# Several waits of TensorE re-arranged at once in a hybrid attention and PEER layer: unrolled head loop, early merge, low halves in quarters, turned choices and h2, the turn of stages 2 and 3

## The reference, cut to what matters

```python
h = rms_norm(x);  z = h @ w_in                    # 2048 -> 9216: GLU a, b, q, k, v, two gates
conv = swish(layer_norm(depthwise_conv31(a * sigmoid(b)))) @ w_conv_out
attn = rms_norm((softmax(q1 k1) - lam * softmax(q2 k2)) @ v) @ w_attn_out     # 8 heads
x = x + (sigmoid(gate_c) * conv + sigmoid(gate_a) * attn) @ w_out
h2 = rms_norm(x)                                  # PEER: 16384 experts of one neuron
idx, sc = top16(top16(q1 . k1) + top16(q2 . k2))  # 8 retrieval heads, 128 x 128 keys
a = einsum("td,thkd->thk", h2, u_tab[idx]);  w = softmax(sc) * gelu(a)
x = x + einsum("thk,thkd->td", w, v_tab[idx])
```

## Time and profile before

| | before |
|---|---|
| three runs, us | 4312.8, 4311.2, 4311.3 (median 4311.3) |
| profiled execution, us | 4312.25 |
| its span, us | 4310.4 |
| mean granted clock of TensorE | 0.972 |
| busy: PE | 4110.0 us, 95% |
| busy: VectorE, GpSimd, ScalarE | 3034.5 (70%), 1442.5 (33%), 1060.9 (25%) |
| DMA | 1225.88 MB, mean 284 GB/s |

### The profile page before, as it was taken

The page is one execution under the profiler, slowest core; times in us unless marked ns, Lnnn a source line. Parts: engine busy times, 40 slices in busy tenths (PEclk is TensorE's granted clock), DMA queues, the critical chain, the costliest instruction groups (busy, mean ns, idle before and its releaser), DMA issues.

```text
span 4310.4 us, 69663 instructions
## 1 busy us (share of the span) xinstructions
PE 4110.0 (95%) x25286; PEld 4014.7 (93%) x25286; DVE 3034.5 (70%) x4447; ACT 1060.9 (25%) x1090; POOL 1442.5 (33%) x682
## 2 busy tenths in 40 slices
PE   8999999999989998999999999999889999999999
PEld 7888888898889998999999999999889999999999
DVE  6876777778756423677637877877468878787874
ACT  3222222222212112222213223232212222222221
POOL 3333232332323332444423333333523323332310
PEclk9999999999999999999979999999999999999999
DMA  7988979979968986866637787778687877777763
GB/s 287 319 310 321 331 273 337 342 261 320 347 223 268 344 309 219 305 224 235 208 137 303 309 317 305 301 309 319 263 315 280 305 287 296 289 294 289 294 255 128
DMA packets 444255, 1225.88 MB, mean 284 GB/s; under 512 B 32800, under 2 KB 256800, under 8 KB 343968
## 3 DMA queue, kind: packets, MB, share of 16 engines
q1 hardware_dynamic: 374224, 881.46, 58.0%
q0 software_dynamic: 36864, 268.45, 15.1%
q10 hardware_dynamic: 32976, 73.47, 4.4%
HBM read 1007.54 MB, written 349.95 MB: 315 GB/s over the span
## 4 chain that ended last, share of the span: by engine, by line
PE 53%; issue 29%; POOL 9%; DVE 6%; DMA 1%; ACT 0%; SPq 0%; POOLq 0%; DVEq 0%; ACTq 0%
PE ST L1710 27%; PE ST L1626 18%; POOL w_lo L551 7%; PE PA L1626 3%; POOL w_lo L543 2%; PE ST L1685 2%; PE PA L1404 2%; PE PA L1636 1%; DVE wk L1234 1%; DMA w_raw<-w_all 1%; DVE cand L1204 1%; DVE wk L1238 0%; DVE isel L1242 0%; DVE ti L1200 0%; DVE wk L1196 0%
## 5 line engine op out<-in xcount | busy, mean ns | idle before, releaser
L624 ACT ACTIVATE w_hi<-w_raw 128x2048 fp32r<-128x2048 f32 x368 | 703.5, 1912 | 1458.5 <-PE ST L1710 786.7
L543 POOL TENSOR_TENSOR w_lo<-w_raw,w_hi 128x2048 fp32r<-128x2048 f32 x133 | 623.8, 4690 | 1154.8 <-ACT w_hi L624 1154.8
L1710 PE MATMUL ST<-wt_hi,w_hi 128*128 128x416 f32 x2048 | 719.4, 351 | 23.3 <-DVE wt_lo L1319 12.7
L1710 PE MATMUL ST<-wt_hi,w_lo 128*128 128x416 f32 x2048 | 724.4, 354 | 0.0
L1710 PE MATMUL ST<-wt_lo,w_hi 128*128 128x416 f32 x2048 | 716.4, 350 | 0.0
L551 POOL TENSOR_TENSOR w_lo<-w_raw,w_hi 128x512 fp32r<-128x512 f32 x280 | 371.4, 1357 | 774.3 <-ACT w_hi L624 774.3
L1404 PE MATMUL PA<-h_hi,w_hi 128*128 128x272 f32 x2496 | 549.4, 302 | 17.8 <-issue 11.8
L581 POOL DMA_INDIRECT rows<-v_rows,v_idx x128 | 312.7, 2443 | 729.5 <-DVE PA L1330 720.8
L1626 PE MATMUL ST<-h_hi,w_hi 128*128 128x416 f32 x1408 | 532.9, 379 | 11.8 <-POOL w_lo L543 11.8
L1404 PE MATMUL PA<-h_hi,w_lo 128*128 128x272 f32 x2496 | 530.0, 295 | 0.0
L1404 PE MATMUL PA<-h_lo,w_hi 128*128 128x272 f32 x2496 | 528.8, 294 | 0.0
(11 more groups left out here) (242 smaller groups left out, 6731.9 us busy)
## 6 DMA issues: line engine op xcount, KB each, us to landing
w_raw<-w_all SPq DMA_DIRECT2D x368, 1024.0 KB
u_in<-w_all SPq DMA_DIRECT2D x128, 1024.0 KB, 8.5
u_rows<-u_out SPq DMA_DIRECT2D x512, 256.0 KB, 7.4
v_rows<-w_all SPq DMA_DIRECT2D x128, 1024.0 KB, 9.1
a_scr<-gb ACTq DMA_DIRECT2D x128, 208.0 KB
g_scr<-g_st ACTq DMA_DIRECT2D x26, 1024.0 KB, 4.4
a_st<-a_scr SPq DMA_DIRECT2D x16, 1664.0 KB
gl_st<-g_scr SPq DMA_DIRECT2D x16, 1664.0 KB, 16.0
```

The source lines that it names most:

```text
L543: pool.tensor_tensor(w_lo[:, slot, :], raw[:, slot, :], w_hi[:, slot, :].bitcast(F32), ALU.subtract)\
L624: act.activation(w_hi[:, slot, :], raw[:, slot, :], ACT.Copy).then_inc(hi_ready, 1)
L1710: last = mm(PD[k], a, r_[b][:, c, :], start=(c == 0 and y == 0), stop=(c == GRP - 1 and y == 2))
```

## The change

1. **Head loop.** TensorE's loop over head pairs and its loops of the merge are written out; its program grows from 5264 rows to 7945. On VectorE a head's last eviction (`evac(hp, r, 8)`) goes ahead of its `o_norm`.
2. **Merge.** The first merge unit does both its tiles for heads 0 to 6, then both for head 7. The first part waits for the eviction of the last `z` unit and the norms of seven heads, the second for the last norm. Head 7's low half is read from `o_lo_st` in place, so one load is gone; the mean stands behind the unit.
3. **Low halves.** All low halves of GpSimd but the first two are made in quarters.
4. **Choices.** `choices_t` stands behind k = 10, `gate_sums` behind k = 3.
5. **Turn of h2.** 64 passes of 128 columns in place of 256 of 32, in two halves, behind unit 40 and in unit 41, into ST. ScalarE copies each half into PA in four operations, for which TensorE waits before the second half and before the rounds.
6. **Turn of stages 2 and 3.** `load_ag(0)` is cut in four parts that stand between the weight loads. Of the last low halves VectorE makes the odd ones and GpSimd the even ones, with 3, 4 and 4 fetches ahead; the `prep` stand between. x2 is no longer loaded ahead of stage 3: group 0 copies its results, x2 is added in group 14 through `gb` (16 loads, `residual`), and in the gather columns at the end (`xg_res`). The row additions of `v` move by three slots.

The diff, cut to its core:

```diff
@@ sync: end of the head loop, end of stage 2, stage 3
-            sp.dma_start(o_lo[:, NH - 1, :].bitcast(F32), o_scr[NH - 1]).then_inc(o_loaded[1], 16)
...
-            load_ag(0)
-            pq_pu_loads(g_end, (NQ + NU) // 2)
+            def load_ag_part(n):
+
+                c, b = slice(2 * n, 2 * n + 2), slice(n * NGB // 4, (n + 1) * NGB // 4)
+                sp.dma_start(a_st[:, c, :], a_scr[c, :, 0:NT].rearrange("c p n -> p c n")).then_inc(ag0_loaded, 16)
+                sp.dma_start(gl_st[:, b, :, :].rearrange("p b c n -> p b (c n)"),
+                             g_scr[b, :, 0:GRP, :].rearrange("b p c n -> p b (c n)")).then_inc(ag0_loaded, 16)
+
+            assert g_end + 3 == (NQ + NU) // 2
+            for v in range(g_end, g_end + 3):
+                for n in range(2):
+                    if 2 * (v - g_end) + n < 4:
+                        load_ag_part(2 * (v - g_end) + n)
+                    sp.wait_ge(lo_ready, v * 2 + (n + 1 + U_PQ))
+                    load_w(v + (U_PQ // 2 + 1), n)
...
-                if n == 0:
-                    sp.wait_ge(unit_done, NZ + NO + NQ + NU)
-                if n < 2:
-                    for i in (2 * n, 2 * n + 1):
-                        sp.dma_start(acc[:, 4 * i:4 * i + 4, :], x2_scr[4 * i:4 * i + 4].rearrange("c p n -> p c n"))\
-                            .then_inc(acc_loaded[i], 16)
+            sp.wait_ge(unit_done, NZ + NO + NQ + NU)
+            sp.dma_start(xg_res[:, :, :], x2_scr[:, :, NT:T].rearrange("c p n -> p c n")).then_inc(xg_loaded, 16)
@@ gpsimd
-            with pool.Fori(1, NZ // 2) as v:
-                for n in range(2):
-                    lo4(v * 2 + n, n)
-            with pool.Fori(NZ // 2, U_PU // 2 + 1) as v:
-                for n in range(2):
-                    lo(v * 2 + n, n)
+            with pool.Fori(1, U_PU // 2 + 1) as v:
+                for n in range(2):
+                    lo(v * 2 + n, n, v * 6 + (3 * n - 3))
...
-            w = U_PU + U_G0 + BU * NGB + 1
-            while w < U_PV + 2:
+            for w, n in ((U_PV - 6, 3), (U_PV - 4, 4), (U_PV - 2, 4), (U_PV, 0)):
+                for i in range(n):
+                    fetch(j)
+                    j += 1
                 pool.wait_ge(lo_ready, w)
-                lo(w, w % 2)
-                w += 1
-                for i in range(2):
-                    if j < SLOTS:
-                        fetch(j)
-                        j += 1
+                nth += 3
+                lo(w, w % 2, nth)
@@ scalar: after the eviction of units 40 and 41
+                act.wait_ge(h2t_ready, n + 1)
+                for q in range(4):
+                    act.activation(PA[:, q, n * 256:n * 256 + 256].rearrange("p (k j) -> p k j", j=32),
+                                   ST[:, 2:4, :].rearrange("p a (k j) -> p (a k) j", j=P)[:, :, 32 * q:32 * q + 32], ACT.Copy)\
+                        .then_inc(h2t_taken, 1)
@@ vector: head loop, rounds, end of stage 2, stage 3
+                    evac(hp, r, 8)
                     o_norm(h)
                     if r == 0:
                         turn(hp, next(turns))
-                    evac(hp, r, 8)
...
-            dve.wait_ge(h2g_ready, 1)
+            dve.wait_ge(h2t_taken, 8)
...
-            for i in range(SLOTS - NGB // 2 * DOTS):
-                dot(NGB // 2, i)
+            for w, dots, preps in ((U_PV - 7, range(0, 3), ()), (U_PV - 5, range(3, 7), ()), (U_PV - 3, range(7, tail), range(0, 3)),
+                                   (U_PV - 1, (), range(3, 8))):
+                split(w, w % 2)
+                if preps and preps[0] == 0:
+                    dve.wait_ge(ag0_loaded, 128)
+                for c in preps:
+                    prep(0, c)
+                for i in dots:
+                    dot(NGB // 2, i)
+            split(U_PV + 1, 1)
@@ tensor: head loop, merge, turn of h2, choices
-            with pe.Fori(0, NH // 2) as hp:
+            for hp in range(NH // 2):
...
+            for ks in (range(KC - 1), range(KC - 1, KC)):
+                for t in range(2):
+                    if ks[0] == 0 and t == 1:
+                        pe.wait_ge(zb_full, NZ + 2)
+                    elif ks[0] > 0 and t == 0:
+                        pe.wait_ge(norm_done, 3 * NH + 1)
+                    for k in ks:
+                        for a, b, f, y in last_head(k):
+                            last = mm(PV[t][:, f, :], a[:, 0, (KC * t + k) * P:(KC * t + k + 1) * P], b,
+                                      start=(k == 0 and y == 0), stop=(k == KC - 1 and y == 2))
+            mean()
+            merge_unit(0, 1, 0, o_hi, o_lows)
...
-                for k in range(KD):
-                    for q in range(4):
-                        for y, src in enumerate((h2_hi, h2_lo)):
-                            last = mm(PA[:, q, 32 * k:32 * k + 32], src[:, k, NT:T].bitcast(F32), ident[:, 32 * q:32 * q + 32],
-                                      start=(y == 0), stop=(y == 1))
-                last.then_inc(h2g_ready, 1)
+                if half == 0:
+                    pe.wait_ge(oh_ready, 1)
+                else:
+                    pe.wait_ge(h2t_taken, 4)
+                for k in range(KD // 2):
+                    for y, src in enumerate((h2_hi, h2_lo)):
+                        last = mm(ST[:, 2 + k // 4, k % 4 * P:(k % 4 + 1) * P], src[:, half * (KD // 2) + k, NT:T].bitcast(F32), ident,
+                                  start=(y == 0), stop=(y == 1))
...
-                u_unit(v_end, 0, UA, {3: choices_t} if tt else None)
-                u_unit(v_end, 1, UA, {1: gate_sums} if tt == TT - 1 else None)
+                u_unit(v_end, 0, UA, {10: choices_t} if tt else None)
+                u_unit(v_end, 1, UA, {3: gate_sums} if tt == TT - 1 else None)
...
-            u_unit(TT * TOPK_UNITS // 2, 1, PD, {KD - 1: h2_turned})
+            u_unit(TT * TOPK_UNITS // 2, 1, PD, {KD - 3: lambda: h2_turned(1)})
+            pe.wait_ge(h2t_taken, 8)
```

More of the change, by code:

```diff
@@ L1334, in _ @@
             own.by(V.memset(acc_g, 0.0))
-            dve.wait_ge(al_loaded, 16)
-            dve.wait_ge(gl_loaded, 16)
-            for c in range(GRP):
-                prep(0, c)
             dve.wait_ge(a_g_ready, 1)
@@ L1343, in _, with group @@
             dve.wait_ge(lo_ready, U_PV + 2)
-            def group(g, parity, more, slots, splits, pre=None):
+            def group(g, parity, more, slots, splits, pre=None, first=False, last=False):
                 s0, rounds, n_slots = slots
@@ L1366, in group @@
                         split(g * GRP + (n + U_PV + 2), n % 2)
-                    if n == GRP - 1 and n_slots > GRP:
+                    if last:
+                        residual(2 * n)
+                        residual(2 * n + 1)
+                    if n == GRP - 1 and n_slots > GRP and not first:
                         gather_add(s0, parity * PER_GRP + GRP, rounds)
             rounds_per = 2 * PER_GRP // NG
-            with dve.Fori(0, NGRP // 2 - 1) as v:
+            group(0, 0, True, (0, 0, PER_GRP - NG), GRP, first=True)
+            group(1, 1, True, (-NG, -1, PER_GRP), GRP)
+            with dve.Fori(0, NGRP // 2 - 2) as v:
                 own.loop(v, 4 * GRP)
                 for b in range(2):
-                    group(v * 2 + b, b, True, (v * (2 * PER_GRP), v * rounds_per, PER_GRP), GRP)
-            own.endloop(NGRP // 2 - 1)
-            done = (NGRP // 2 - 1) * 2 * PER_GRP
+                    group(v * 2 + (b + 2), b, True, (v * (2 * PER_GRP) + (2 * PER_GRP - NG), v * rounds_per + (rounds_per - 1), PER_GRP), GRP)
+            own.endloop(NGRP // 2 - 2)
+            done = (NGRP // 2 - 1) * 2 * PER_GRP - NG
             def hand_over():
```

103 lines of the change are left out of this document (66 added, 37 removed).

## The result

| | before | after |
|---|---|---|
| runs, us | 4312.8, 4311.2, 4311.3, 4317.85 | 4209.0, 4223.6, 4219.7, 4201.8 |
| median, us | 4312.05 | 4214.35 |
| profiled execution, us | 4312.25 | 4208.99 |
| span, us; mean granted clock | 4310.4; 0.972 | 4206.9; 0.984 |

The ratio is 0.9761 with an interval of 0.9744 to 0.9777. Forecast were 4214 us, and 4180 to 4248. The total is right; the parts show that this is partly luck, as misses of either sign cancel. The runs of the changed kernel lie 22 us apart, those of before 7: one more thing to explain.

The account below looks back on a forecast made before the run. TensorE was taken to bound the kernel, busy 4110.0 of 4310.4 us, so the sum is one of stalls plus the turn of h2: -16 - 14 + 20 - 20 - 36 - 31 = -97, from 4311.3 to 4214 us, range 4180 to 4248.

Parts of the forecast that it names:

- Point 1: Head loop: writing it out removes three waits for instructions and their slow clock; late `o_norm` gives back 2 us; minus 16.
- Point 2: Merge: begun with seven heads, 84 of 96 matmuls stand ahead of what needs the last head; minus 14 us.
- I charge 3 us: Start of the merge: TensorE wants the first gated tile at about 1222.5 and gets it at about 1225.
- Point 3: Low halves in quarters: GpSimd and VectorE take turns, so low halves come late in the top-k stage; plus 20 us.
- Point 4: Top-k stage: choices at k = 10, seven steps later, remove four waits for `isel` and their slow clock; minus 20 us.
- Point 5: Turn of h2: 64 passes of 128 columns replace 256 of 32, with a 4 us wait for ScalarE; minus 36 us.
- rival (c): Turn of h2 stays at half clock by the skill's transpose rule: 6.7 us more and some, 4222 us; chance 0.05.
- Point 6: Turn of stages 2 and 3: loads in parts, `prep` between dots, recover most of 41 us lost; minus 31 us.
- Rival (b): End of stage 2 stays bound by DMA: 15 to 20 us more, 4232 us; chance 0.14.
- (a): Top-k stage: low halves in quarters keep up, so their cost is 0; time 4194 us; chance 0.22.
- (d): Head loop: written out, instruction fetching still waits at each head pair; time 4230 us; chance 0.05.
- (e): Rounds of stage 2: quartered low halves come late, making the kernel slower, 4339 us at 11 us each; chance 0.03.

Follow-up runs that it names:

- the last kernel: Changed kernel with low halves whole from the first w_out unit on, last dots ahead of the prep, and load_ag(1) in four parts: median 4192.4 us, ratio 0.97.

## Why the prediction was right, point by point

| point | forecast, us | first profile | mean of profiles |
|---|---|---|---|
| 1 head loop | -16 (10 to 18) | -15.9 | -16.2 (of two before) |
| 2 merge, seven heads | -14 (9 to 18) | | -9.6 (one pair) |
| 3 quarters, top-k | +20 (0 or 20) | +14.2 | +19.9 |
| 3 quarters, merge | none | | -11.0 (one pair) |
| 4 choices | -20 (16 to 20) | | -21.3 (one pair) |
| 5 turn of h2 | -36 (32 to 42) | -38.5 | -38 |
| 6 turn of stages (236 to 248) | -31 (16 to 35) | -24.1 | -22.6 |
| 6 stage 3 proper (from 248) | none | +2.1 | +6.1 |

The last column adds up to -92.7, with +1 for the rest, where the ratios say -103 and -95.

**Point 1** held in its mechanism and size. The written-out code is fetched without a wait. That the eviction ahead costs the heads 2 us can't be seen: 1125.1 us with it behind is inside the range with it ahead. The two profiles with the loop as before (1134.2, 1140.3) lie 6 us apart, so the size is known to a few us only.

**Point 2** was right about the place: the stretch shrank by 15.4 us, 1.4 more than forecast, and the last norm's end was covered. But the step "I charge 3 us" for the gates took the stretch for the stage. VectorE's work is a chain of its own here, and TensorE caught up with it: without quarters 9.6 us are left of it at the end of the merge. With quarters in place its parts came to 4.8 us for the seven heads and 3.9 for the eviction, by one profile each.

**Point 3** was right in the top-k stage: turns are taken, `cand` takes 2.6 us in place of 5.9, and three or all four `wk` operations of a tile take 3.25 to 3.45 us, where before one took 4.27 and three 2.29. In most tiles two to three low halves are late, not one as the list of signs had it. I had them late by 3.4 and 0.4 us a tile; they are by 1.4 in some tiles and 3.2 in others. The step that failed is the sum's last line on quarters, where I looked for their price only where TensorE waits for a low half. Where it waits for VectorE they are a gain, and in the merge that is half of the stage's gain. This miss (11 to the good) and those of points 2 and 6 (4.4 and 14.5 on the mean, to the bad) cancel for the most part, which is why the total came out so near. That is luck.

**Point 4**: "seven steps later is enough" is right with whole low halves. "Points 3 and 4 cancel" came out as 19.9 - 21.3. But they aren't a plain sum: with quarters in place k = 10 is worth some 5.7 us by one profile. That both hide behind the same lateness of TensorE fits the shorter waits for `isel` (1.9 in place of 3.6 us), but was not tested by itself.

**Point 5**: the wait for ScalarE was 3.8 us (forecast 4) and the passes took 0.112 us each (0.105), 64 of them some 7.2 us by their starts, at a granted clock of 1.00. So rival (c) falls. The rule of the Trainium skill's page TensorE: Matmul & The Clock Gate, Part 4: PE-mode transpose, that full clock doesn't engage, is about transpose mode. These are ordinary matmuls against an identity, so it is not tested here. The reading "at half clock throughout" of the old passes was wrong: in the kernel before too they ran at full clock (0.112 us each) for their first 5.9 us, and the mean of 0.56 hid it. The sum stands, as it took their length from the row.

**Point 6** named the right thing as late next (the last part, three `prep`, a dot, the fetch, the low half) and had it late by 4 us where it was 13.6. The clock took less than the 4 us charged: it was at half for 17 us, but for all but 5.5 of these TensorE stood in the wait, and 447 matmuls took 87.0 us for work of 84.7 (an estimate by the 443 matmuls in 83.9 us and four of 0.189). The waits before stage 3 came to 14.5 us, where the prediction's signs had them under 12. The step that failed is "lands about when VectorE wants it": it landed 10.5 us later. Rival (b), bound by DMA, is half right: order brought back 13 us of it on the mean (9 in the last kernel), and 331 GB/s with a weight load of 16.5 us still ends last there. The second step that failed is "nothing there" for stage 3: it has a gap of 3.8 us behind the weight load that follows `load_ag(2)`, and one of 1.9 in group 14, where VectorE waits for x2 in `gb`, a load of 12.85 us. Stage 3 is 6.1 us longer on the mean, some two fifths of this point's miss.

**Rivals.** (a) would have been the case with whole halves; (d) falls with the head loop's 16 us; (e) falls: low halves in the rounds took 5.05 us on the median and 5.45 at most, far from 7.8.

What stays open: why the head loop's length varies by 8 us between profiles (the waits for `e` move); what decides whether one or two operations of VectorE get in; and what makes stage 3's matmuls 0.6% quicker in two profiles. No run has `load_ag(1)` in parts without the dots first, `load_ag(2)` in parts, or x2 loaded as before, and none takes the other parts of point 6 one by one.

## What to carry to other kernels

Where the operations of two engines take turns, as GpSimd's low halves and VectorE's operations do here, cutting the longer instruction in pieces moves the wait from one engine to the other. Do it where the other engine is the one that the bound engine waits for (here the merge, -11 us), and leave it whole where the cutting engine's own result is wanted (here the top-k stage, +19.9); one setting for the whole kernel gave both away. A stretch's gain is not the stage's: after each removed wait look whether the same engine catches up with another queue some tens of us later. And when bulk loads stand ahead of paced ones in a queue, cut them all: with only the first cut the wait moved to the next (7.1 us), and with two cut one of 3.5 us was left behind the third.

## What the runs showed of the hardware that was not expected

GpSimd's quarter and VectorE's two-operand operations over SBUF take turns: the quarter's median is 1.29 us and its maximum 3.35 us, most of one `wk` operation (2.29) more. `isel`, a reduction of one operand, was never lengthened: 2.29 us in every tile of every kernel, also inside a run of quarters. The Trainium skill's page SBUF — State Buffer, section Who interferes with whom, says the same of such a reduction on trn2, and the trace agrees.

A pass into 32 columns costs as much as one into 128, 0.112 us at full clock. 256 of the narrow ones in a row lost the full clock with no wait ahead of them (0.55 over 50.2 us), while two times 32 passes of 128 columns between ordinary matmuls kept it (1.00). Whether the width does it or the length of the row is not shown: the narrow ones, too, kept it for their first 5 us, and each row of wide ones lasts 3.6.
